# Retention in three sweeps over all tiles, its tables formed in the opening

## The reference, cut to what matters

```python
lg = jnp.log1p(-jnp.exp(p['ret_log_decay']))           # per direction and head
decay  = where(diff >= 0, exp(lg * max(diff, 0)), 0)   # 128 x 128
scores = einsum('bhncd,bhnmd->bhncm', qc, kc) * decay
inner  = einsum('bhncm,bhnme->bhnce', scores, vc)
zeta, xi = exp(lg * (C - 1 - pos)), exp(lg * (pos + 1))
chunk_kv = einsum('bhnmd,bhnme,hm->nbhde', kc, vc, zeta)
step = lambda s, kv: (exp(lg * C) * s + kv, s)         # lax.scan over tiles
cross  = einsum('bhncd,nbhde,hc->bhnce', qc, s_prev, xi)
o = inner + cross                                      # forward + backward
o = o * rsqrt(mean(o * o, -1) + EPS);  ret = silu(g) * o
```

## Time and profile before

| | us |
|---|---|
| three runs | 4037.79, 4043.84, 4041.14 (median 4041.14) |
| profiled execution | 4045.88 |
| its span, first to last instruction | 4044.1 |
| PE busy | 3640.5 (90% of the span) |
| DVE, ACT, POOL busy | 2219.8, 1464.6, 1083.0 |
| granted TensorE clock, mean | 0.944 |

### The profile page before, as it was taken

How to read it: one execution, slowest core, us unless ns; L and a number is a source line. 1 busy time by engine, 2 the same in 40 slices (tenths; PEclk the granted TensorE clock), 3 DMA queues, 4 the chain that set the end, 5 groups by cost and what they waited for, 6 DMA issues and landing times. The chain is left out here.

```text
span 4044.1 us, 53514 instructions
## 1 busy us (share of the span) xinstructions
PE 3640.5 (90%) x19724; PEld 3066.5 (76%) x19724; DVE 2219.8 (55%) x3988; ACT 1464.6 (36%) x2965; POOL 1083.0 (27%) x963
## 2 busy tenths in 40 slices
PE   7979975988779899999999899759897889999997
PEld 3668975777667788888888679758786778888886
DVE  5478345766676544444444583357676744554554
ACT  2331124666623522222222411247674342222222
POOL 1121110111100044444554421101111004554554
PEclk9989977999989999999999899779998999999999
DMA  5345200000144101111110261000004411111111
GB/s 193 125 157 181 64 4 29 1 14 32 39 157 164 42 27 36 41 41 41 41 31 31 88 205 49 3 27 6 37 6 156 151 42 42 47 55 44 42 55 54
DMA packets 150807, 263.16 MB, mean 65 GB/s; under 512 B 8824, under 2 KB 120585, under 8 KB 148202
## 3 DMA queue, kind: packets, MB, share of 16 engines
q1 hardware_dynamic: 143532, 211.59, 15.7%
q0 software_dynamic: 5776, 44.04, 2.7%
q10 hardware_dynamic: 1328, 5.24, 0.4%
HBM read 227.79 MB, written 33.06 MB: 65 GB/s over the span
## 5 line engine op out<-in xcount | busy, mean ns | idle before, releaser
L2777 POOL TENSOR_TENSOR x<-x,mlp_tmp 128x512 f32<-128x512 f32 x576 | 785.6, 1395 | 1323.1 <-DVE mlp_tmp L2758 1318.1
L2758 DVE TENSOR_TENSOR mlp_tmp<-psum,gate 128x512 f32<-128x512 f32 x576 | 391.7, 689 | 273.2 <-POOL x L2777 194.6
L152 PE MATMUL psum<-act_hi,w_hi 128*128 128x512 f32 (+1 forms) x1280 | 472.7, 369 | 14.1 <-DVE w_lo L2736 14.1
L153 PE MATMUL psum<-act_lo,w_hi 128*128 128x512 f32 (+1 forms) x1280 | 472.3, 369 | 0.0
L154 PE MATMUL psum<-act_hi,w_lo 128*128 128x512 f32 (+1 forms) x1280 | 472.0, 369 | 0.0
L152 PE MATMUL psum<-w_hi,hidden_hi 128*128 128x512 f32 x1152 | 449.8, 390 | 0.0
L153 PE MATMUL psum<-w_lo,hidden_hi 128*128 128x512 f32 x1152 | 448.4, 389 | 0.0
L154 PE MATMUL psum<-w_hi,hidden_lo 128*128 128x512 f32 x1152 | 448.2, 389 | 0.0
L2750 DVE TENSOR_TENSOR hidden_lo<-square,hidden_hi 128x512 fp32r<-128x512 f32 x160 | 102.3, 640 | 592.0 <-ACT hidden_hi L2722 592.0
L2714 ACT ACTIVATE relu<-psum 128x512 f32<-128x512 f32 x160 | 88.9, 555 | 666.1 <-PE psum L154 666.1
L1728 DVE TENSOR_REDUCE att_max<-psum 128x1 f32<-128x512 f32 (+2 forms) x272 | 217.8, 801 | 180.0 <-PE psum L154 179.8
(11 more groups left out here) (363 smaller groups left out, 8119.5 us busy)
## 6 DMA issues: line engine op xcount, KB each, us to landing
w_raw<-in_mlp_w SPq DMA_DIRECT2D x128, 512.0 KB, 3.8
side_w<-in_w_ada SPq DMA_DIRECT2D x40, 1024.0 KB, 6.4
w_raw<-in_w_in SPq DMA_DIRECT2D x32, 512.0 KB, 4.8
hy_ahead<-in_hy_ahead POOLq DMA_DIRECT2D x8, 2048.0 KB, 12.2
ada_w<-in_w_ada SPq DMA_DIRECT2D x8, 1024.0 KB, 26.1
open_tab<-in_hy_ahead POOLq DMA_DIRECT2D x8, 1024.0 KB, 17.3
spec_scratch<-open_staged SPq DMA_DIRECT2D x16, 512.0 KB, 2.7
hy_spec<-spec_scratch SPq DMA_DIRECT2D x16, 512.0 KB, 3.5
```

Of the source, the lines that this page charges most:

```text
L152: pe.matmul(out, lhs[0], rhs[0], start=start, stop=False)
L153: pe.matmul(out, lhs[0], rhs[1], start=False, stop=False)
L2758: dve.tensor_tensor(tmp[:, j % 2, :], ps[:, 4 + j % 4, :], gate[:, int(t >= LAT_TILES), 512 * h:512 * h + 512], ALU.mult).then_inc(gated.s ...
L2777: pool.tensor_tensor(a, a, tmp[:, j % 2, :], ALU.add).then_inc(added.sem, 1)
```

## The change

In retention, the tables move to the opening: `zeta`, `xi`, `gcol` of both layers stay in small tiles, and the mask goes through a scratch tensor in device memory (`ret_dm_dram`) and is loaded back at the start of each retention block. The rest is three sweeps:

```diff
+            for i in range(ALL_TILES):
+                key_values(i)
+            for n in range(nt + 1):
+                if n < nt:
+                    turn(n)
+                if n:
+                    score(n - 1)
+            for p in pairs:
+                total(p)
+                if p >= 2:
+                    turn_back(p - 2)
+            turn_back(pairs[-2])
+            turn_back(pairs[-1])
```

```diff
+            def key_values(i):
+                t = kv_order[i]                     # [8, 9, 7, 0, 6, 1, 5, 2, 4, 3]
+                pe.wait_ge(k_scaled.sem, k_scaled[t])
+                if i >= 4:
+                    pe.wait_ge(kv_moved.sem, kv_moved[kv_order[i - 4]])
...
+            def turn(n):
+                pe.wait_ge(q_scaled.sem, q_scaled[n])
                 if n >= 2:
+                    pe.wait_ge(moved.sem, moved[n - 2])
+                for a in range(4):                  # two heads of q or of k at a time
+                    pe.transpose(ps[:, 2 * (n % 2) + 1, a * C:(a + 1) * C], ret[:, n, a * P:(a + 1) * P], kit.ident[:])
                 for h in range(H):
+                    last = pe.transpose(ps[:, 2 * (n % 2), h * C:(h + 1) * C], qx[:, n, h]..., kit.ident[:])
...
+            def score(n):
+                pe.wait_ge(moved.sem, moved[n])
+                pe.wait_ge(kv_moved.sem, ...) if n < 2 else pe.wait_ge(masked.sem, masked[n - 2])
+                for h in range(H):
+                    rows = slice(h % 2 * RET_D, (h % 2 + 1) * RET_D)
+                    last = pe.matmul(ps[:, 4 + 2 * (n % 2) + h % 2, at:at + C], qkT[rows, n, 1, h // 2], qkT[rows, n, 0, h // 2], ...)
...
+            def total(p):                           # 2 tiles, 4 heads, 2 products each
+                pe.wait_ge(masked.sem, masked[nt - 1])
+                if p >= 4:
+                    pe.wait_ge(y_ready.sem, y_ready[p - 4])
...
+            def turn_back(p):
+                pe.wait_ge(y_ready.sem, y_ready[p])  # 4 transposes
...
+            act.activation(rs[:, 4, 0:1], kit.ones[:, 0:1], ACT.Sqrt)
+            for n in tiles:
+                act.activation(qkT[:, n]..., ps[:, 2 * (n % 2) + 1, :], ACT.Copy)
+                act.activation(qxT[:, n]..., ps[:, 2 * (n % 2), :], ACT.Copy).then_inc(moved.sem, 1)
...
+            for p in pairs:                          # ACT
+                act.activation(o2[:, p % 2]..., sum_bank(p), ACT.Square).then_inc(squared.sem, 1)
+                act.wait_ge(meaned.sem, meaned[p])
+                act.activation(rs[:, 1, c], rs[:, 0, c], ACT.Sqrt).then_inc(rooted.sem, 1)
...
+            def state(i):                            # DVE, forward
+                for h in range(H):
+                    last = dve.scalar_tensor_tensor(out=st[r, fwd[i + 1], h], in0=st[r, fwd[i], h], scalar=gcol[r, h:h + 1],
+                                                    in1=kv[r, fwd[i], h], op0=ALU.mult, op1=ALU.add)
...
+            for p in pairs:                          # DVE: reduce, mean, root's inverse, scale, gate
+                norm(p)
```

In the opening the conditioning's weights go first. POOL loads its tables only when chunks 6 and 7 have landed; ACT issues chunks 1, 3 and 5:

```diff
+            chunk_load(sp, 0)
+            chunk_load(sp, 2)
+            sp.dma_start(w3_raw[:], io["hy_w3"]).then_inc(w3_in.sem, 16)
+            chunk_load(sp, 4)
+            sp.dma_start(decay[:, 0:2 * K], io["hy_decay0"]).then_inc(d_in.sem, 16)
+            sp.dma_start(decay[:, 2 * K:], io["hy_decay1"]).then_inc(d_in.sem, 16)
...
+            sp.dma_start(kit.ident[:], io["ident"]).then_inc(small_in.sem, 16)
...
+            log_decays()                              # DVE, 31 small instructions
+            for c in range(3):
+                reduce_argument(0, c)
+            dve.wait_ge(small_in.sem, small_in[3])
+            for c in range(3):
+                dve.wait_ge(sined.sem, sined[(0, c)])
+                reduce_argument(1, c)
+                add_bias(c)
...
             pool.memset(kit.ones[:], 1.0).then_inc(ones_set.sem, 1)
+            for c in (n_chunks - 2, n_chunks - 1):
+                pool.wait_ge(w_in[c % RING].sem, w_in[c % RING][c])
```

More of the change, by code:

```diff
@@ L380, in _ @@
             pe.wait_ge(cond_ready.sem, cond_ready["cond"])
-            for c in range(3):
-                second(c)
             chunk(0)
+            second(0)
             chunk(1)
+            second(1)
+            second(2)
+            chunk(2)
+            chunk(3)
+            chunk(4)
             pe.wait_ge(sined.sem, sined[(1, 2)])
@@ L440, in even_part @@
                 act.activation(even[:, f[1]], ps[:, 4 + 2 * (n % 2):6 + 2 * (n % 2), :], ACT.Copy).then_inc(even_out.sem, 1)
-            for g in tiles_of[units[0]]:
+            retention_tables()
+            for l in range(DEPTH):
+                powers(l)
+                high(tiles_of[units[0]][l])
+            for g in tiles_of[units[0]][DEPTH:]:
                 high(g)
@@ L954, in in_first_loads @@
         sp.dma_start(raw[:, n, :, 0:w], w_dram[:, 4 * h:4 * h + 4, c0:c0 + w]).then_inc(kit.sig(f"proj_raw{n}", 16).sem, 16)
+    if l == 0:
+        for i in range(2):
+            sent = kit.sig(f"spec_sent{i}", 16)
+            sp.wait_ge(sent.sem, sent.total)
     if l:
@@ L1191, in phase_retention @@
[L1191 to L1202 removed]
+        s.plan(kv_order)
@@ new lines, in _ @@
+            dve.memset(st[r, fwd[0]], 0.0).then_inc(st_f.sem, 1)
+            for t in kv_order:
+                k = ret[:, t, RET_W:2 * RET_W].rearrange("p (h e) -> p h e", h=H)
+                dve.tensor_tensor(kz[:, t], bcast(k, 2, 2), bcast(zeta, 3, RET_D), ALU.mult).then_inc(k_scaled.sem, 1)
+            for n in range(AHEAD):
+                q_scale(n)
+            state(0)
+            dve.wait_ge(dm_in.sem, dm_in[0])
+            for n in tiles:
+                if n + AHEAD < nt:
+                    q_scale(n + AHEAD)
+                state(n + 1) if n < 8 else None
+                mask(n)
@@ L1424, in _ @@
-            for n in range(nch + 2):
-                if n < nch:
+                pe.wait_ge(masked.sem, masked[nt - 1])
+                if p >= 4:
+                    pe.wait_ge(y_ready.sem, y_ready[p - 4])
+                for i in range(2):
+                    n = 2 * p + i
+                    for h in range(H):
+                        out = sum_bank(p)[:, (i * H + h) * RET_D:(i * H + h + 1) * RET_D]
+                        pe.matmul(out, pT[:, n, h], values(n, h), start=True, stop=False)
+                        last = pe.matmul(out, qxT[:, n, h], st[:, n, h], start=False, stop=True)
```

574 lines of the change are left out of this document (284 added, 290 removed).

## The result

The changed kernel takes 3980.61 us (median of 4 runs, 3976.2 to 3984.15), the kernel before 4042.15 us. The ratio is 0.984, 95% interval 0.9828 to 0.9852: 61.5 us faster, where 118 were forecast. The time lies 23 us above the range.

The account below looks back on a forecast made before the run. PE is busy for 90% of the span, so time is to be had only where it waits or runs at its lower clock. Gains 50.5 + 53.8 (retention, two layers) + 13.9 (opening) = 118.2 give 3923 us; range 3900 to 3958.

Parts of the forecast that it names:

- Step 2: Key-values of layer 0's retention: 9.4 us at the 2.4 GHz level, ending at 10.5 us from the block's start.
- Step 5: Sums by pairs of tiles in retention: 32 instructions x 0.117 = 3.75 us a total, pitch 4.25 with the turn back.
- rival (a): Clock falls in the 64-column stretches: key-values alone 3939 us, totals alone 3952, both 3968; chance 0.23 together.
- step 4: Tile sweep of retention: DVE 2.0 us a tile, nobody waits for a result of the same tile, pitch 2.2 against 4.33.
- a chain across three engines: Old tile loop of layer 0's retention: 4.33 us a tile, DVE waiting for PE's transposes, PE for copies and mask.
- The opening: Before the first projection: first reduction at 9.8, first fold 7.9 us earlier at 70.4, some 6 at the end; 13.9 gained.
- Rival (b): Opening gives little: small inputs late or sines delayed, the 7.9 us gain becoming 0 or a loss of 2; chance 0.11.
- Sweep, states and pairs: Retention: pitch 2.2 us a tile, forward states 0.7 a tile, 4.25 a pair; blocks of 60.5 and 51.9 us.
- The store's wait: End of each retention block: the store's 4.9 us no longer waited for, lying under the latent attention's norm.
- Silu's table load: The gate's Silu adds one table load of 1.28 us a layer on ACT in the projection, hidden.
- The rule on transposes: Tile sweep: the page's rule would keep it at the lower clock; the prediction held that the rows speak against it.
- rival (c): Tile sweep stays at the lower clock: pitch 4.2 us, + 36, 3959 us, near 4004 with rival (a); chance 0.03.

Follow-up runs that it names:

- kv128b: Changed kernel with key-value products of 128 columns instead of 64, but for one head of the two context tiles; 3971.96 us.
- totfill: Changed kernel with 16 transposes without use between the last scores and the first sum; 3948.75 us.
- kv128_fill: Changed kernel with both the 128-column key-values and the 16 useless transposes between last scores and first sum; 3943.15 us.
- gapleft: Changed kernel with 16 useless transposes ahead of the last scores, so PE's wait for the last mask stays; 3963.91 us.
- ln_first: Changed kernel with ACT's logarithm in the opening taken before it issues the weights of chunks 1, 3 and 5; 3981.96 us.
- small_first: Changed kernel with bias, gain and ident loaded before the weights of chunks 0 and 2 in the opening; 3970.96 us.
- all_early: Changed kernel with the edits of kv128_fill, ln_first and small_first together; 3933.04 us.
- no_mask: Changed kernel without the decay mask's arithmetic in the opening, the mask being a constant; 3979.16 us.
- after: The changed kernel itself, as profiled, against the kernel before; 3980.61 us, ratio 0.984.
- totmix: Changed kernel with one useless 128x128 transpose behind each head's two products in the sums, but for a pair's last head; 3990.65 us.
- tot128: Changed kernel with products of 128 columns instead of 64 in the sums, the extra results not read; 3957.85 us.
- score_order: Changed kernel with a tile's four score products in head order 0, 2, 1, 3 instead of 0, 1, 2, 3; 3980.9 us.

## Why the prediction was wrong

The direction was right; the size was off by a factor of two. It failed at three of its steps.

- **Step 2, the clock in the key-values ("I take the high level: end at 10.5").** 17.2 us at clock 0.50, +7.8. I took the short gap ahead for harmless. The row that mattered was shown: in the earlier trace rows PE was busy for 17.5 us with this very kind of product and stayed at 0.50. I had read it as the cost of the long idle time before it. The missing half: once at 0.50, the clock did not come back within a stretch of 64-column products in any run, while with 128 columns it did (kv128b). The two prices were right (9.14 us where the clock stayed up, 17.2 where it fell). Which of them comes true is not settled by the gap of 1.59 us, which was the same each time.
- **Step 5, the clock in the sums (32 x 0.117 = 3.75 a pair).** 6.8 us a pair, +15.4 us in layer 0. The earlier trace rows shows sums at 1.00, but they came out of a loop already at that level in which PE did not wait at all. I priced this as rival (a) and gave it 0.23. It came true in both stretches and both layers: 3968 by its own sum. totfill and kv128_fill show that the lower clock in the sums is the loss and that work put ahead of them takes it away, 8 times of 8. That the waits on the last masks trigger the fall is argued, not shown: gapleft kept one and the clock held in layer 0. That PE would wait there was to be seen in my own step 4: DVE's 2.0 us a tile stood beside PE's 2.0, and PE has to wait for the last mask in any case.
- **The reading of the old loop ("a chain across three engines", PE "waits for the copies").** In the old loop of layer 0 DVE waited for PE, but PE waited for nobody. The kernel before, in the middle of that loop (columns as in the earlier trace rows):

```profile
580.00:590.00 10.00, 10.00 (x85) 9.25 (x84) 4.46 (x7) 2.91 (x6) 0.00 (x0) 1.00 0.00 0
```

So the old loop was bound by PE at the full clock, 10 x 4.33 = 43 us, and the forecast for sweep and sums together (22 + 21) is no less. The new loops took 20 + 35 = 55 us in layer 0. What the block gained came from the tables, the states and the end.

- **The opening ("the first reduction at 9.8", "that is 27 us", "I take 29.3").** -13.9 forecast, +2.0 measured. The first reduction was 5.7 us late through ACT's issuing, which I had not put on ACT's list although the diff has the three loads ahead of the logarithm. This cost next to nothing in itself, as ln_first shows (taps(0) 0.45 us earlier without it). The small inputs landed 5.4 us later than at 323 GB/s: in 0 to 33 us the traffic was 297 GB/s, and SP needed 7.63 us to issue one decay table. small_first shows this at 7.7 us, of which 4.1 lie ahead of the taps and the rest in the taps and chunks at the lower clock behind them. From the taps to the first fold it took 36.4 us, 31.1 in all_early: 5 of the 7 us too much are again the clock (among them 3.75 instead of 1.99 for taps(0) and 5.51 instead of 3.62 for the chunk behind it). The mask, which I had allowed for, costs nothing (no_mask). At the end 6 us were forecast and 2.2 came: x's squares waited 5.45 us for their load and ended at 210.7, beside the spectra, so the statistics were late on their own. Rival (b) had the right place and too small a size: a fold up to 2 us later than before, against 4.2 (and its times should read 3931 to 3933, not 3935).
- **What held.** Sweep, states and pairs: with the clock up in the sums, the blocks took 59.7 and 52.2 us against 60.5 and 51.9. Part of this fit is offset: layer 0's key-values still began at the lower level (10.7 us against 9.4), and the tile pitch was 1.98 us, bound by DVE, not 2.2; states 0.86 us for four (0.7 forecast). The store's wait is gone, and the latent norm behind it takes 22.2 us as before (22.0). Silu's table load stands inside the projection at 448.04, and ACT's copies there still waited for PE, 105.9 us in layer 0 (106.6 before): hidden, as forecast.
- **The rule on transposes.** In the tile sweep some 60% of PE's time goes to transposes (1.02 of 1.67 us a tile), and the clock was 1.00:

```profile
556.00:569.00 13.00, 12.92 (x124) 10.71 (x124) 12.89 (x39) 8.30 (x17) 0.73 (x1) 1.00 0.00 1
```

In layer 1 of kv128_fill the clock was back behind sixteen transposes alone, and in the changed kernel itself it came back at 555.4, behind the 16 transposes that follow the key-values from 551.76 on. The 64-column products showed nothing of the kind. The Trainium skill, "TensorE: Matmul & The Clock Gate", section "Part 4: PE-mode transpose", says that the full clock does not engage for transposes. These rows contradict it for fp32 transposes here, and rival (c) fell with it. Transposes among other work are no guarantee either: before, the loop of layer 1, 12 transposes a tile among 64-column sums, ran 16 us at 0.50 (third line of the earlier trace rows).

The rest of the miss, from 3968 to 3981, is the opening, less what the faster sweep gave back. The range ended at 3958 because it took in rival (a) "but for its worst"; its worst was what happened.

## What to carry to other kernels

Splitting a loop into sweeps puts all short products into one stretch. Ask at which clock level PE will enter that stretch, and what it has to wait for just before: the sums of layer 0 cost 15 us too much here, because the clock fell behind waits of a microsecond and did not come back in the stretch. If a product's time does not grow with its columns, wider operands or a few useless transposes ahead are worth a trial. In an opening, list what each engine issues ahead of its first short instruction; and where two waits stand in a row, removing the first alone gives next to nothing (ln_first). And compare the clock of stretches that an edit did not touch before its total is believed: 8 us came and went in the key-values of unchanged code.

## What the runs showed of the hardware that was not expected

- fp32 products with 64 and with 128 columns take the same time per instruction at the 2.4 GHz level: 0.109 to 0.117 us.
- A stretch of 64-column products that was at 0.50 stayed there: 34 us in the sums (after), also with a transpose behind every fourth one (totmix). One at 1.00 could stay (184 instructions in totfill, 9.14 us in gapleft) or fall 2.4 us in with no new wait (small_first, layer 0, 15.13 us). With 128 columns the clock came back within the stretch (tot128, kv128b).
- The clock fell behind waits of 0.9 to 2 us, with no long idle time near. The same wait was followed by a fall or not: 0.9 us in gapleft's two layers, 1.59 us ahead of the key-values in all runs. What decides between the two stays open.
- A score of four heads takes 0.71 us where operands are taken from both halves of the partitions, 1.16 where all stand in one half. Their order did not matter (score_order); the cause stays open.
- Issuing is not free: three loads of 1 MB kept ACT for 8.47 us, while SP issued others beside it, and one of 1 MB kept SP for 7.63 us.
